# Feed-forward group ends: the last low half moves from GpSimd to VectorE, and two search steps move forward

## The reference, cut to what matters

```python
x = x + g1 * (y @ w_out[l])                       # "output columns"
h = rms_norm(x, norm2_g[l]) * (1.0 + sc2) + sh2
a, gate = split(h @ w_up)                         # 2 x 2816 features
a = causal depthwise conv (width 3)(a) + conv_b
x = x + g2 * ((gelu(a) * gate) @ w_down)
return rms_norm(x, final_g)
```

## Time and profile before

| | |
|---|---|
| median of three runs | 1272.58 us |
| profiled execution | 1272.06 us |
| its span on the core | 1270.0 us, so 2.06 us lie around it |
| TensorE (matmul) busy | 1214.0 us, 96% |
| VectorE busy | 707.0 us, 56% |
| ScalarE busy | 579.5 us, 46% |
| GpSimd busy | 622.6 us, 49% |
| mean granted TensorE clock | 0.982 |

### The profile page before, as it was taken

How to read it: one execution, slowest core, us unless ns; L and a number is a source line. 1 busy time by engine, 2 the same in 40 slices (tenths; PEclk the granted TensorE clock), 3 DMA queues, 4 the chain that set the end, 5 groups by cost and what they waited for, 6 DMA issues and landing times.

```text
span 1270.0 us, 17299 instructions
## 1 busy us (share of the span) xinstructions
PE 1214.0 (96%) x5814; PEld 1005.2 (79%) x5814; DVE 707.0 (56%) x1406; ACT 579.5 (46%) x997; POOL 622.6 (49%) x315
## 2 busy tenths in 40 slices
PE   6898999987899999999999999999999999999997
PEld 5687788866788888888878887888888888888876
DVE  5944877987866898989983433353522111111223
ACT  5245666655843444234423665552544134422443
POOL 0045755874314355445545666334355445544555
PEclk8899999998999999999999999999999999999999
DMA  8657663550123122232224443324222222322223
GB/s 309 201 182 253 183 197 104 167 149 25 43 87 113 50 100 100 99 109 90 99 99 141 133 141 131 135 75 151 74 100 99 93 92 97 99 99 99 92 98 141
DMA packets 58664, 153.92 MB, mean 121 GB/s; under 512 B 6600, under 2 KB 20296, under 8 KB 58608
## 3 DMA queue, kind: packets, MB, share of 16 engines
q1 hardware_dynamic: 47760, 135.64, 31.2%
q10 hardware_dynamic: 10848, 17.57, 4.3%
HBM read 142.66 MB, written 10.52 MB: 121 GB/s over the span
## 4 chain that ended last, share of the span: by engine, by line
PE 42%; issue 24%; POOL 15%; DVE 11%; ACT 3%; DMA 3%; SPq 1%; ACTq 0%; POOLq 0%; DVEq 0%
PE ps L1916 10%; PE ps L1917 10%; PE ps L1919 10%; POOL w_lo L575 10%; DVE unread L1378 4%; POOL act_lo L732 3%; PE ps L2207 2%; DMA w_ada<-in_w_ada 1%; PE ps L1895 1%; PE ps L1896 1%; PE ps L1940 1%; PE ps L2196 1%; PE ps L2186 1%; PE ps L1900 1%; PE ps L1842 1%
## 5 line engine op out<-in xcount | busy, mean ns | idle before, releaser
L575 POOL TENSOR_TENSOR w_lo<-w_raw,w_hi 128x1024 fp32r<-128x1024 f32 x148 | 354.8, 2398 | 436.0 <-ACT w_hi L748 436.0
L1916 PE MATMUL ps<-h_hi,w_hi 128*128 128x512 f32 x896 | 354.9, 396 | 2.9 <-POOL w_lo L584 2.9
L1917 PE MATMUL ps<-h_lo,w_hi 128*128 128x512 f32 x896 | 350.2, 391 | 0.0
L1919 PE MATMUL ps<-h_hi,w_lo 128*128 128x512 f32 x896 | 331.4, 390 | 0.0
L748 ACT ACTIVATE w_hi<-w_raw 128x1024 fp32r<-128x1024 f32 x148 | 156.8, 1059 | 335.9 <-PE ps L1919 328.1
L1916 PEld LDWEIGHTS ps<-h_hi,w_hi 128*128 128x128 f32 x896 | 168.9, 188 | 38.1 <-POOL w_lo L584 3.7
L1919 PEld LDWEIGHTS ps<-h_hi,w_lo 128*128 128x128 f32 x896 | 168.4, 188 | 36.1
L1917 PEld LDWEIGHTS ps<-h_lo,w_hi 128*128 128x128 f32 x896 | 169.0, 189 | 32.4
L1780 DVE SCALAR_TENSOR_TENSOR ps<-conv_in,conv_w,ps 128x512 f32<-128x512 f32 x44 | 33.2, 754 | 207.2 <-ACT ps L1161 207.2
L1916 PE MATMUL ps<-act_hi,w_hi 128*128 128x512 f32 x352 | 140.2, 398 | 5.0 <-POOL act_lo L732 2.6
L1919 PE MATMUL ps<-act_hi,w_lo 128*128 128x512 f32 x352 | 137.6, 391 | 0.0
(11 more groups left out here) (262 smaller groups left out, 1856.5 us busy)
## 6 DMA issues: line engine op xcount, KB each, us to landing
w_raw<-in_w SPq DMA_DIRECT2D x173, 512.0 KB, 3.2
w_ada<-in_w_ada SPq DMA_DIRECT2D x48, 512.0 KB, 4.3
x_sb<-in_x SPq DMA_DIRECT2D x4, 1024.0 KB, 9.8
q_st<-qk_dram SPq DMA_DIRECT2D x32, 128.0 KB, 4.1
out<-fin_o ACTq DMA_DIRECT2D x14, 256.0 KB, 2.1
qi_st<-qi_dram ACTq DMA_DIRECT2D x18, 128.0 KB, 4.7
qk_dram<-qk_hi ACTq DMA_DIRECT2D x4, 512.0 KB, 2.7
qk_dram<-qk_lo ACTq DMA_DIRECT2D x4, 512.0 KB, 3.7
```

The lines of the kernel that those rows point to most:

```text
L575: pool.tensor_tensor(r(w_lo[:, slot]), w_raw[:, slot], w_hi[:, slot], ALU.subtract).then_inc(w_lo_ready, 1)
L1916: pe.matmul(ps[:, bank], r(hi_t[:, kk]), r(xh(kk)), start=(i == 0), stop=False)
L1917: pe.matmul(ps[:, bank], r(hi_t[:, kk]), r(xl(kk)), start=False, stop=False)
L1919: mm = pe.matmul(ps[:, bank], r(lo_t[:, kk]), r(xh(kk)), start=False, stop=last_k)
```

## The change

The low half of the last activation tile of every group is taken out of GpSimd's program (its loop is one round shorter and the last two tiles are written out, the order of the rest is kept). VectorE makes it in `last_act_lo`, called right behind the last `up`: it waits for GpSimd's low half before it and for `act_hi`, and subtracts. In the first half this stands in front of the search pieces or, in the third group, in front of the `memset` of `sum2` and `late_soft(28)`.

In the output columns of the first half the search budget rises from 2.0 to 2.7 per column, and behind the last two columns there is none. In the last `up` of groups 0 and 1 the budget ahead of `act_f` falls from 2.2 to 1.2.

```diff
--- before.py
+++ after.py
@@ -717,19 +717,28 @@
                                 late_masked_bias(FIRST_LATE + 2 * f + j + 1)
                                 n = nu + 2 * f + j + 2
                                 w_lo_unit(n % 2, n + 1)
-                            pool.wait_ge(act_hi_ready, F + f + 1)
-                            pool.tensor_tensor(r(act_lo[:, f]), act_f[:, f % 2], act_hi[:, f], ALU.subtract).then_inc(act_lo_ready, 1)
+                            if f < nf - 1:
+                                pool.wait_ge(act_hi_ready, F + f + 1)
+                                pool.tensor_tensor(r(act_lo[:, f]), act_f[:, f % 2], act_hi[:, f], ALU.subtract).then_inc(act_lo_ready, 1)
                         for k in range(KD):
                             if 2 * nf + k + 1 < FIRST_LATE:
                                 late_masked_bias(FIRST_LATE + 2 * nf + k + 1)
                             w_lo_unit((nd + k + 2) % 2, nd + k + 3)
                         continue
-                    with pool.Fori(0, nf // 2, 1) as i:
+                    with pool.Fori(0, nf // 2 - 1, 1) as i:
                         for u in range(2):
                             for j in (2, 3):
                                 w_lo_unit((nu + j) % 2, nu + j + 1 + 2 * u + 4 * i)
                             pool.wait_ge(act_hi_ready, F + 1 + u + 2 * i)
                             pool.tensor_tensor(r(act_lo[:, u + 2 * i]), act_f[:, u], act_hi[:, u + 2 * i],
+                                               ALU.subtract).then_inc(act_lo_ready, 1)
+                    for f in range(nf - 2, nf):
+                        for j in (2, 3):
+                            n = nu + 2 * f + j
+                            w_lo_unit(n % 2, n + 1)
+                        if f < nf - 1:
+                            pool.wait_ge(act_hi_ready, F + f + 1)
+                            pool.tensor_tensor(r(act_lo[:, f]), act_f[:, f % 2], act_hi[:, f],
                                                ALU.subtract).then_inc(act_lo_ready, 1)
                     pairs(nd, KD // 2)
             pool.wait_ge(rms_kept, 2)
@@ -1722,6 +1731,13 @@
                     dve.scalar_tensor_tensor(out=r(y_lo[:, g]), in0=ps[:, Y_BANKS[h][i]], scalar=mix_g[:, g:g + 1],
                                              in1=y_hi[:, g], op0=ALU.mult, op1=ALU.subtract).then_inc(norm_lo, 1)
 
+                def last_act_lo(F, nf):
+
+                    dve.wait_ge(act_lo_ready, F + nf - 1)
+                    dve.wait_ge(act_hi_ready, F + nf)
+                    dve.tensor_tensor(r(act_lo[:, nf - 1]), act_f[:, (nf - 1) % 2], act_hi[:, nf - 1],
+                                      ALU.subtract).then_inc(act_lo_ready, 1)
+
                 def column(n, o, bank, gate, q, sq=0):
 
                     dve.wait_ge(unit_done, n + 1)
@@ -1748,7 +1764,8 @@
                     for g in range(KD):
                         column(base + g, x2[:, g], 2 + g % 2, mod[:, gate + g:gate + g + 1],
                                (q0 + g, g % 2) if q0 else None)
-                        search_for(us)
+                        if not q0 or g < KD - 2:
+                            search_for(us)
 
                 dve.wait_ge(x2_loaded, 16 * (h + 1))
                 if h == 0:
@@ -1756,7 +1773,7 @@
                     dve.tensor_scalar(found_bound.bitcast(I32), kept[:].bitcast(I32), 0, None, ALU.bitwise_or).then_inc(state_back, 1)
                     dve.wait_ge(state_back, 1)
                     unread = unread_of[1]
-                    columns_beside_search(nb, 2 * KD, s0 - KD, 2.0)
+                    columns_beside_search(nb, 2 * KD, s0 - KD, 2.7)
                 else:
                     root(2)
                     vlink(dve.memset(sum2[:], 0.0))
@@ -1797,11 +1814,14 @@
                         with dve.Fori(0, nf // 2, 1) as i:
                             for u in range(2):
                                 up(F + u + 2 * i, f0 + u + 2 * i, u, nu + 2 + 2 * u + 4 * i)
+                        last_act_lo(F, nf)
                         column_loop(nd, 5 * KD, s0 if g == 2 else 0)
                         continue
                     if g < 2:
                         for f in range(nf):
-                            up(F + f, f0 + f, f % 2, nu + 2 + 2 * f, lambda: search_for(2.2))
+                            up(F + f, f0 + f, f % 2, nu + 2 + 2 * f, lambda: search_for(2.2 if f < nf - 1 else 1.2))
+                            if f == nf - 1:
+                                last_act_lo(F, nf)
                             search_for(4.6)
                         columns_beside_search(nd, 5 * KD, 0, 3.6)
                         continue
```

## The result

The changed kernel took 1263.03 us in the median of 6 runs (1262.21 to 1266.56), the kernel before 1273.1 us beside it (6 runs, 1270.53 to 1277.54). The ratio is 0.9915 (95%: 0.9889 to 0.9940). The profiled executions are closer together: 1264.89 us (span 1262.9, mean granted clock 0.985) against 1272.06 us (span 1270.0, clock 0.982), which is 7.2 us where the sum said 6.9.

The account below looks back on a forecast made before the run. TensorE, busy 96% of the span, was taken as the bound, so only its stalls and low-clock time count. 0.8 + 1.3 + 0.6 + 0.6 + 1.7 + 1.9 = 6.9 us off 1272.06 gave 1265.3 us, range 1262.5 to 1268.3.

Parts of the forecast that it names:

- three 8-tile ends: At three group ends with 8 tiles, TensorE's 0.27 us stall for act_lo goes: 0.8 us in all.
- group 1, first half: At this 8-tile group end, TensorE's 1.34 us stall for act_lo goes: 1.3 us.
- group 2, second half: At this 6-tile group end, act_lo comes earlier: 0.6 us won, 1.0 us of stall left.
- group 2, first half: At this 6-tile group end, act_lo comes earlier: 0.6 us won, 1.4 us of idle time left.
- clock behind it: Behind group 2 of the first half, the drop to half clock goes as TensorE idles less: 1.7 us, or nothing.
- transition of the first half: From output columns to up units, moving search pieces away removes TensorE's idle time and clock drop: 1.9 us.
- The wait for GpSimd: At group ends, VectorE's act_lo waits for GpSimd's w_lo and ends 0.6 us behind it.
- the rival of no wait: At group ends VectorE doesn't wait for GpSimd, so 6-tile ends win 2.4 us more: 1262.9 us; chance 10%.
- the rival of the late VectorE: In the first half's output columns, the bigger budget makes VectorE late and the clock still drops: 1266.7 us; chance 12%.
- the rival with 24%: The clock still drops in group 2 of the first half, only 5.2 us are won: 1267.0 us; chance 24%.
- The slow rival: In group 2 of the first half, the delayed chain behind late_soft(28) holds TensorE up: 1274.2 us; chance 4%.
- How the numbers follow: Closing step: chances of forecast and rivals turned into the range, 1262.5 to 1268.3 us, and faster 0.49, same 0.48, slower 0.03.

Follow-up runs that it names:

- experiment 4: The changed kernel with each group's last product written in place in PSUM, so VectorE's subtraction has one SBUF input: 1262.16 us, ratio 0.9926 to the kernel before.
- Experiment 8: The changed kernel with a search budget of 3.9 instead of 2.7 in the first six output columns: 1273.04 us, one execution.
- its repeat: After "the kernel after": the changed kernel unedited, timed again, 1265.97 us, ratio 0.9955. After "before": the kernel before unedited, timed again, 1272.23 us.
- part 1 alone: The kernel before with only the last low halves moved to VectorE, output-column search pieces left as they were: 1266.53 us, ratio 0.9973.
- experiment 9: The changed kernel with the search budget of 2.2 kept in the last up of groups 0 and 1, instead of 1.2: 1265.37 us, one execution.
- 10: The changed kernel with four more memsets of sum2 on VectorE ahead of late_soft(28) in group 2 of the first half: 1267.87 us, one execution.
- part 2 alone: The kernel before with only the output-column search pieces moved (budget 2.7, none behind the last two columns), low halves left on GpSimd: 1269.76 us, ratio 0.9979.
- experiment 1: The kernel before, unedited, timed once more against itself: 1272.23 us against 1271.91 us, ratio 1.0014.

## Why the prediction was right or wrong

The steps of the sum, forecast against the table of shifts:

```
step                                    forecast   measured
three 8-tile ends                         0.8       0.83
group 1, first half                       1.3       1.34
group 2, second half                      0.6       0.67
group 2, first half                       0.6       0.69
clock behind it                           1.7       1.57
transition of the first half              1.9       2.11 (2.36 by its first up matmul)
all                                       6.9       7.21 of 7.68
```

The other 0.5 us is small steps of 0.04 to 0.16 us that follow the stalls and went with them.

**The wait for GpSimd: right.** The forecast was an end of 0.6 us behind the `w_lo`; it is 0.55. The trace shows it, experiment 4 shows on what it depends, and the rival of no wait is out. Had it been taken as a whole instruction behind (0.69), each 6-tile end would have won 0.5, not 0.67 to 0.69.

**The transition: right, and a little too small.** The second half was the pattern (0.48 us idle, 18.57 us); the changed first half has 0.47 us and 18.36 us. The margin on VectorE was forecast as about 1 us and is 0.92, in part by luck: the terms of the prediction make 3.4 - (2.4 - 0.60) = 1.6 us. In the trace column 6 starts 2.3 us behind a pace of 5.44 us a column, so nothing of the 0.60 us was to be had. Experiment 8 shows the rival of the late VectorE, one piece further.

**The clock behind group 2: right in outcome, wrong in kind.** I took the drop to go since 1.6 us idle was nearer to 1.44, which had none. With the same 0.20 + 1.4 us idle at this place the kernel after, its repeat and part 1 alone have no drop; experiments 8, 9 and 10 have one, worth 1.6 us in 8 and 9. The idle time of 0.20 + 2.05 us (before, its repeat, part 2 alone) was followed by one each time. So between the two it is a matter of chance in these traces, three of six. That the changed kernel itself has the drop in some of its executions, the rival with 24%, is likely by this and not shown: neither of its two traces has it. The term should have been 1.7 times a chance, not 1.7 or nothing.

**The slow rival: right mechanism, wrong place.** Its price did not fall due. But its margin is 0.65 us at the matmuls of `late_logits(29)`, and not 1 us at the `w_lo` of down unit 2, which has 789.42 - 787.99 = 1.43 us. I had followed only ScalarE's chain behind `late_soft(28)`, and not who waits for the banks that it reads.

**The small budget.** I gave it the gain at group 1, which it doesn't need: experiment 9 has no stall there. It saves 0.8 us in group 0, where I had said that the columns drain any delay. Part 2 alone takes 1.04 of the 1.34 us at group 1. And the late `act_hi` was only half of what was wrong there: GpSimd's subtraction was also held for 0.5 us beside VectorE, which I had read over.

**The number itself: out of the range by 0.7 us, by the first comparison.** No step of the sum failed by this much: the traces give 7.7 us, and 1272.58 - 7.7 = 1264.9. The step that failed is "How the numbers follow". Its range was made of the prices of mechanisms alone, and the sum took a small part of 0.5 us for the way from the profiled execution to the median. By how much two sets of executions of the same program differ was put at nothing. The runs show that it is more than the 0.7 us: two comparisons of the same two kernels gave 10.1 and 5.9 us. In the part in front of the edit the traces differ by -1.5 to +0.9 us, at the same program text, and the clock drops there fall in other places.

Most of what moved the changed kernel between its two sets, 2.9 us, goes with the clock. In the first six executions the granted clock was 0.983 to 0.988 (median 0.985), in the twelve of the repeat 0.976 to 0.986 (median 0.982), and five of those had 0.980 or less and took 1268.1 to 1270.5 us. At the 0.85 us for 0.001 of experiment 1, the 0.003 between the medians make an estimated 2.6 us. Why the first six had the higher clock stays open, and so do the 1.2 us by which the before moved, since its first six executions have no clock on record. By the repeat alone the time would be 1272.58 x 0.9955 = 1266.9, inside the range.

## What to carry to other kernels

Where one engine is busy 96% of the time, list its idle places and its clock drops one by one, and price each: that sum came out within 0.8 us of the trace. When an elementwise step is moved to VectorE beside a busy GpSimd, give it an operand in PSUM: it took 0.69 us, against 2.4 with both in SBUF. Small filler work comes in whole pieces (here 1.26 us), so a budget is right or wrong by a piece; and a difference of less than 1% needs more than one comparison, since these two differed by 4 us.

## What the runs showed of the hardware

- The wait of VectorE for GpSimd's instruction isn't for the whole of its own: the rest behind it is 0.55 us for 512 columns, where 0.69 us is the time alone, and that at all 36 group ends of six traces (0.54 to 0.55), whether the subtraction began early or late in the `w_lo` (2.4 or 1.01 us long). So some 0.14 us of it no longer has to be done then.
- It also goes the other way. A GpSimd instruction that came second was held by VectorE's: 2.83 us instead of 2.38. Kernel after, GpSimd in group 2 of the first half, beside the `act_lo` of VectorE that ends at 780.06; then the kernel before, GpSimd behind the pair of the earlier trace rows, 3.35 us instead of 2.40:

```profile
779.47 2.83 POOL L679 TENSOR_TENSOR bias_m<-bias_m,score 128x1024 f32<-128x1024 f32 x1
...
87.92 3.35 POOL L584 TENSOR_TENSOR w_lo<-w_raw,w_hi 128x1024 fp32r<-128x1024 f32 x1
```

- A one-input step of VectorE (`score<-score`, 128x768, SBUF to SBUF) took 1.46 us beside a `w_lo` (experiment 9; 1.39 in the kernel before) and 0.56 us with GpSimd idle (kernel after).
- A clock drop behind group 2 of the first half was worth 1.57 to 1.60 us (kernel before, experiments 8 and 9), and the same idle time there (0.20 + 1.4 us) was followed by one in 3 of 6 traces. With 1.95 us of filler matmuls in the stall there was none, in the one trace that tried it.
